# A two-layer model and a hybrid block on one core: who adds the third weight sum of the FFNs' Strassen pairs

## The reference

```
def swiglu(u, w_in, w_out):
    gt, up = jnp.split(u @ w_in, 2, axis=-1)
    return (jax.nn.silu(gt) * up) @ w_out      # u 256x1024, w_in 1024x5632, w_out 2816x1024
```

## Time and profile before

| | |
|---|---|
| median of 3 runs | 1032.86 us |
| the profiled execution | 1034.49 us, span 1032.6 us |
| TensorE (PE) | busy 1025.4 us, 99% |
| VectorE (DVE) | busy 870.8 us, 84% |
| ScalarE (ACT) | busy 614.9 us, 60% |
| GpSimd (POOL) | busy 33.2 us, 3% |
| granted TensorE clock | full in every slice |
| accumulating transfers (L637) | 9 of 1 MB, 12.1 us to land in the median |

### The profile page before, as it was taken

The page is one execution under the profiler, slowest core; times in us unless marked ns, Lnnn a source line. Parts: engine busy times, 40 slices in busy tenths (PEclk is TensorE's granted clock), DMA queues, the critical chain, the costliest instruction groups (busy, mean ns, idle before and its releaser), DMA issues.

```text
span 1032.6 us, 13375 instructions
## 1 busy us (share of the span) xinstructions
PE 1025.4 (99%) x4848; PEld 834.4 (81%) x4848; DVE 870.8 (84%) x1378; ACT 614.9 (60%) x925; POOL 33.2 (3%) x39
## 2 busy tenths in 40 slices
PE   9999999999999999999999999999999999999998
PEld 8877788888878888788888788787778888888886
DVE  6877888979789987888797888989979878897976
ACT  6745465656665656656566664638657446565663
POOL 1221000000000000000000000000000000000000
PEclk9999999999999999999999999999999999999999
DMA  8762496777456544877775453444454469677733
GB/s 289 222 208 82 136 287 179 243 212 252 118 184 184 183 131 135 258 191 224 224 240 168 158 169 123 157 152 149 156 159 136 148 191 296 175 248 211 256 99 123
DMA packets 140459, 192.42 MB, mean 186 GB/s; under 512 B 12732, under 2 KB 82874, under 8 KB 140266
## 3 DMA queue, kind: packets, MB, share of 16 engines
q1 hardware_dynamic: 134130, 178.36, 53.8%
q0 software_dynamic: 5856, 12.64, 6.3%
q10 hardware_dynamic: 408, 0.56, 0.3%
HBM read 181.03 MB, written 1.05 MB: 176 GB/s over the span
## 4 chain that ended last, share of the span: by engine, by line
PE 91%; DVE 5%; DMA 2%; ACT 1%; issue 1%; SPq 0%; DVEq 0%
PE ps L2225 11%; PE ps L2230 11%; PE ps L2226 11%; PE ps L2242 7%; PE ps L2243 7%; PE ps L2247 7%; PE ps L2367 5%; PE ps L2372 5%; PE ps L2369 5%; PE ps L2210 3%; PE ps L2208 3%; PE ps L2209 3%; DVE wlo L1228 2%; PE ps L2301 1%; PE ps L2317 1%; DMA raw<-in_a_w_in 1%
## 5 line engine op out<-in xcount | busy, mean ns | idle before, releaser
L1228 DVE TENSOR_TENSOR wlo<-raw,whi 128x1024 fp32r<-128x1024 f32 (+2 forms) x266 | 320.9, 1232 | 26.6 <-ACT whi L666 25.5
L666 ACT ACTIVATE whi<-raw 128x1024 fp32r<-128x1024 f32 (+2 forms) x265 | 269.9, 1052 | 99.1 <-DMA raw<-in_ffn_w_in 28.2
L2225 PE MATMUL ps<-whi,ath 128*128 128x512 f32 (+1 forms) x588 | 234.7, 400 | 0.4
L2226 PE MATMUL ps<-whi,atl 128*128 128x512 f32 (+1 forms) x588 | 227.4, 388 | 0.0
L1242 DVE TENSOR_TENSOR wlo<-work,whi 128x1024 fp32r<-128x1024 f32 x126 | 147.6, 1218 | 14.4 <-ACT whi L685 14.4
L2230 PE MATMUL ps<-wlo,ath 128*128 128x512 f32 (+1 forms) x588 | 156.1, 387 | 0.0
L685 ACT ACTIVATE whi<-work 128x1024 fp32r<-128x1024 f32 x126 | 125.3, 1051 | 26.5 <-DMA work<-work 19.4
L2225 PEld LDWEIGHTS ps<-whi,ath 128*128 128x128 f32 x588 | 110.5, 188 | 29.2 <-issue 5.2
L2230 PEld LDWEIGHTS ps<-wlo,ath 128*128 128x128 f32 x588 | 109.4, 188 | 23.4 <-DVE wlo L1228 0.4
L2226 PEld LDWEIGHTS ps<-whi,atl 128*128 128x128 f32 x588 | 110.6, 188 | 21.0 <-issue 0.5
L2242 PE MATMUL ps<-whi,brh 128*128 128x512 f32 x272 | 106.9, 393 | 0.1
(11 more groups left out here) (405 smaller groups left out, 1512.4 us busy)
## 6 DMA issues: line engine op xcount, KB each, us to landing
raw<-in_w_in SPq DMA_DIRECT2D x104, 256.0 KB, 2.9
work<-in_ffn_w_in SPq DMA_DIRECT2D x96, 256.0 KB, 5.5
raw<-in_ffn_w_out SPq DMA_DIRECT2D x88, 256.0 KB, 4.3
raw<-in_ffn_w SPq DMA_DIRECT2D x84, 256.0 KB, 3.8
raw<-in_ffn_w_in SPq DMA_DIRECT2D x80, 256.0 KB, 3.7
raw<-in_a_w_in SPq DMA_DIRECT2D x48, 256.0 KB, 4.4
raw<-in_b_w_in SPq DMA_DIRECT2D x48, 256.0 KB, 3.1
work<-in_ffn_w SPq DMA_DIRECT2D x48, 256.0 KB, 5.5
```

The source lines that it names most:

```text
L666: a_(unit_view(whi, slot, w), unit_view(raw, slot, w), ACT.Copy).then_inc(hi_ready, 1)
L1228: v_.tensor_tensor(unit_view(wlo, slot, w), unit_view(raw, slot, w), unit_view(whi, slot, w), ALU.subtract).then_inc(lo_ready, 1)
L2225: mm(ps[bk + apart * t][:, 0:w], ath[:, k, t * P:(t + 1) * P], rh[:, kk, :], start=k == 0, stop=False)
L2226: mm(ps[bk + apart * t][:, 0:w], atl[:, k, t * P:(t + 1) * P], rh[:, kk, :], start=False, stop=False)
```

## The change

The accumulating transfer goes. In its place GpSimd adds b22 to t3's place itself, in two instructions of 1024 columns, one for each half. The semaphore counts them one by one, and ScalarE waits for the half that it is about to read and not for both. The waits ahead of the adds are the same as they were ahead of the transfer.

```diff
-ACC_ROW = 2048
...
-        def t3_there(n, k):
+        def t3_there(n, k, half):
 
-            return 16 * (len(PAIRED) * n + k + 1)
+            return 2 * (len(PAIRED) * n + k) + half + 1
...
                     pool.wait_ge(sem("pair_sums"), sums_done(n, f"{k}_t1"))
                     pool.wait_ge(part_loaded["b22"], parts_there(n, k, "b22"))
-                    nc.gpsimd.dma_start(pair_whole("t3"), pair_whole("b22"), accum_op=ALU.add, max_dma_last_dim=ACC_ROW)\
-                        .then_inc(sem("pair_t3_added"), 16)
+                    for half in range(2):
+                        t3 = pair_part(f"t3_{half}")
+                        nc.gpsimd.tensor_tensor(t3, t3, pair_part(f"b22_{half}"), ALU.add).then_inc(sem("pair_t3_added"), 1)
...
                 elif name == "t3":
-                    act.wait_ge(sem("pair_t3_added"), t3_there(n, k))
+                    act.wait_ge(sem("pair_t3_added"), t3_there(n, k, half))
```

## The result

The changed kernel takes 1037.95 us (median of 4 runs, 1037.54 to 1038.82) beside 1032.95 us of the kernel before (4 runs, 1032.62 to 1033.26): a ratio of 1.0049, with a 95% interval of 1.0034 to 1.0064. It is 5.0 us slower; the forecast was 6.8 us slower, at 1039.7.

What follows compares the result with a forecast made beforehand. TensorE, busy 1025.4 of 1032.6 us, was taken as the bound. Transfers 0, first pairs 1.7 and later pairs 5.1 gave +6.8 us: 1039.7 us for the median, range 1032.3 to 1046 (forecast case's own 1037 to 1042).

Steps and rivals of the forecast that it cites:

- What goes: Nine accumulating transfers of 1 MB in the pair stages: removing them is worth 0 on TensorE's path.
- What an add costs: Each pair's two GpSimd adds hold VectorE's SBUF-with-SBUF work for 2 x 2.24 us; 40 us at stake over nine pairs.
- One sign: Expected in the changed kernel's trace: 18 GpSimd adds of 2.3 to 3.7 us.
- Second and third pairs: Six later pairs of the FFNs: the split behind t2 makes TensorE 0.65 to 1.0 us late each, 5.1 us together.
- The pair named as the tightest: Second pair of the second FFN: TensorE's matmul had only 1.9 us of room at the split behind t2.
- First pairs: First pair of each of three FFNs: brl makes TensorE 0.55 us late each, 1.7 us together.
- Rival 2: Nine pair stages: the adds' cost is hidden from TensorE; 1032.9 us, give or take 1; chance 0.23.
- the chance hole of the second FFN: TensorE's 2.3 us hole near 583, behind a down unit's late weights; the forecast credited nothing for it.
- rival 1: After t1, GpSimd's add wins against a running split, stretching it; 11 us or 17 us slower; chance 0.25.
- Hidden: Rival 2: in the pair stages TensorE loses nothing to the adds; 1032.9 us, give or take 1; chance 0.23.
- Faster: Weight loads freed from the transfers' queue, the hole near 583 closes, adds cost TensorE nothing; 1030.6 us; chance 0.07.

Runs made afterwards that it cites:

- the one with zeros: The changed kernel with GpSimd writing zeros over both halves of t3 instead of adding b22: 1033.72 us, ratio 1.0002 to the kernel before.
- half: The changed kernel with every GpSimd add taking only the first 512 of its 1024 columns: 1033.96 us, ratio 1.0003 to the kernel before.
- moved: The changed kernel with second and third pairs' adds waiting until the split behind t2 is written: 1033.74 us, ratio 1.0003 to the kernel before.
- first pairs alone: The changed kernel without the third weight sum in second and third pairs, GpSimd adding only in the three first pairs: 1033.09 us, ratio 0.9997.
- 2048 columns: The changed kernel with one GpSimd add of 2048 columns per pair in place of two: 1037.25 us, ratio 1.0038 to the kernel before.
- the last experiment: The changed kernel with each half added twice, four GpSimd adds a pair with a wait between: 1063.3 us, ratio 1.0298 to the kernel before.

## Why the prediction was right

**What goes: right.** The transfer was worth 0 on TensorE's path; without transfer and adds the ratio is 0.9999.

**What an add costs: right.** A pair's adds were to hold VectorE for 2 x 2.24 us; the trace has 2.27 and 2.28 from handover to the end, and 1.08 us for a split behind an add. That inputs in PSUM escape shows in both kernels; that only reading excludes shows in the one with zeros. VectorE lost 29.7 us of the 40 at stake. The rest would have fallen on its idle time and on instructions with a PSUM input; this was not added up. One sign was missed: the adds were to take 2.3 to 3.7 us each, and they took 2.99 to 4.47, the longest where both splits of a first pair went ahead.

**Second and third pairs: right in the mechanism and the sum, less so by place.** Predicted 5.1 us in six waits of 0.65 to 1.0; the weight loads waited 5.5 us in six stops, at the very split. The first of the pairs had 0.57 us at the matmul. The pair named as the tightest (second of the second FFN) had 0.7 us, and the last, with 2.8 us of room by the rows before, had 1.5. In the two pairs with the longest waits, 1.0 and 1.5 us, GpSimd had waited for b22 and VectorE stood idle 1.01 us for ScalarE's high part, and neither falls on the pair where the kernel before had b22 late. So which pair is tight changed from trace to trace, and the near agreement of the sums is partly luck. The adds were not back to back here either; the split behind t2 lies behind both of them in any order, and so its lateness is the same.

**First pairs: wrong, and the wrong term of the sum.** The step took "the two adds back to back: nothing stands between them on POOL's queue" and had brl 0.55 us late in each, 1.7 us in all. The runs show 0 (1033.09 with adds in first pairs alone). In the trace the engines take turns after each instruction even with no wait between the adds, or the first add comes in only behind both splits; either way brl is in time. The second was the rule: it happened in 17 of the 18 first pairs in the traces of the six kernels whose first pairs have adds (changed, half, moved, first pairs alone, 2048 columns, twice). So two things that the step took for granted failed, that the add gets in as soon as the first split ends, and that nothing comes between the adds. The Trainium skill (GPSIMD Engine Reference, Instruction dispatch) says that each Pool core starts the next instruction as soon as its own share of the last one is done; the trace shows that VectorE gets its inputs between two such adds all the same. Rival 2 had a turn between the adds as one of its two branches.

**The sum.** 5.5 us of waits in the profiled execution, less 1.6 us by which the chance hole of the second FFN was shorter (2.3 before, 0.7 after), is 3.9; the span grew by 4.1 us, from 1032.6 to 1036.7. The medians differ by 5.0. The forecast of 6.8 is over that by 1.8 us, which is the 1.7 of the first pairs.

**The rivals.** GpSimd winning against a running split: in no pair of the changed kernel; the first split after t1 kept its 1.22 us in all nine, as at 207.60 and in the two first pairs shown, and rival 1 needed it stretched. The exception at 62.70 in the earlier trace rows comes back in every trace, the changed kernel's among them, where GpSimd's add is recorded from 63.90:

```profile
63.50 3.91 DVE L1227 TENSOR_TENSOR wlo<-raw,whi 128x1024 fp32r<-128x1024 f32 x1 [0.53 <-ACT whi L665]
```

So it is real, and its cause stays open; a transfer, a change of POOL's configuration and a first use of the add stand just ahead of it on POOL's queue, which nothing here separates. Hidden: refuted by the time. Faster: refuted, taking the transfer away gave nothing back (0.9999).

**Open.** Which of two waiting engines gets the inputs: two first pairs with the same distance between split and add (0.17 us) went two ways. Why the add goes behind both splits in nearly all first pairs, but takes its turn between a split and t2, is open too. And why each further us of hold in the last experiment cost 0.6 us was not taken apart by place, beyond the share of the clock.

## What to carry to other kernels

Before work goes from VectorE to GpSimd, look at what VectorE has queued at that moment: if those instructions read two SBUF operands, an add of 1024 columns on GpSimd takes up to 2.3 us out of VectorE (in this kernel), and VectorE would have done it in 1.15. It is free only where the next consumer has more room than that, so put such an add behind the tight split and ahead of a known gap, or let VectorE do it; moving it by one semaphore wait took the 5 us back. A transfer that only an engine with idle time waits for (ScalarE, 19.4 us) is not a cost, even with a landing time of 12 us, and none of the variants tried beat the kernel before.

## What the runs showed that was not expected

- GpSimd's and VectorE's turns alternate instruction by instruction with no semaphore between two adds: 208.82, 211.09, 212.17, 214.45, 216.59.
- VectorE's second of two splits in a row can go ahead of a GpSimd add that has waited since before the first ended (452.26 to 454.45), and in another pair doesn't (163.32 to 164.37).
- A GpSimd fill of 128x1024 f32 takes 0.96 us, beside 2.40 for an add, and leaves VectorE alone.
- With waits of 2.5 to 2.6 us in TensorE's work, three of them in the last experiment had the granted clock at its lower level for 3.4 us; waits of the same length elsewhere in that trace (221.19) did not.
